# A decoder trunk on one core: input projection and low parts in another order, first two experts' rows by one-hot products, tables of slots later

## What is computed

```python
mod = silu(c) @ W_ada + b_ada                   # 6 x 1024: shift, scale, gate of both halves
h = rmsnorm(x) * (1 + scale1) + shift1
z = h @ W_in                                    # 4096 columns: q, k, v, pooled input, two gates
q, k = rmsnorm of each head of 64
A = block-sparse causal attention(q, k, v) @ W_attn_up
B = windowed means (2/4/8/16) minus the token, a linear map per group
x = x + gate1 * ((sigmoid(ga) * A + sigmoid(gp) * B) @ W_out)
h = rmsnorm(x) * (1 + scale2) + shift2
group = top-1 of 4;  expert pair = top-2 of the 8 in it      # routing of every token
x = x + gate2 * sum over 2 chosen experts of weight * (silu(h @ w1) * (h @ w3)) @ w2
```

## Time and profile before

| | us |
|---|---|
| median of 3 runs (lowest to highest) | 644.74 (643.94 to 645.98) |
| the profiled execution's own time | 648.95 |
| its span in the trace | 647.2 |
| PE busy | 579.7 (90% of the span) |
| DVE, ACT, POOL busy | 305.1, 161.3, 114.7 |
| bytes moved by DMA | 173.82 MB, mean 269 GB/s |

### The profile page before, as it was taken

The page is one execution under the profiler, slowest core; times in us unless marked ns, Lnnn a source line. Parts: engine busy times, 40 slices in busy tenths (PEclk is TensorE's granted clock), DMA queues, the critical chain, the costliest instruction groups (busy, mean ns, idle before and its releaser), DMA issues.

```text
span 647.2 us, 7332 instructions
## 1 busy us (share of the span) xinstructions
PE 579.7 (90%) x2786; PEld 343.2 (53%) x2786; DVE 305.1 (47%) x580; ACT 161.3 (25%) x348; POOL 114.7 (18%) x156
## 2 busy tenths in 40 slices
PE   3899699999999999999999999999986968889791
PEld 1554477777766677777788834333332323333241
DVE  0229876546646565249545385332221222253257
ACT  3034012234433434353303202121111111111110
POOL 3022242069300000064001011111111111101000
PEclk9899999999999999998999989999997988889897
DMA  8995944302581506030685695999999999999863
GB/s 308 396 353 212 338 159 163 131 19 111 201 319 52 210 1 260 1 131 0 265 337 244 235 386 177 369 423 418 419 420 422 419 422 419 420 419 421 337 276 130
DMA packets 42648, 173.82 MB, mean 269 GB/s; under 512 B 6396, under 2 KB 6460, under 8 KB 30836
## 3 DMA queue, kind: packets, MB, share of 16 engines
q1 hardware_dynamic: 35280, 159.40, 62.4%
q0 software_dynamic: 5744, 12.84, 5.4%
q10 hardware_dynamic: 1588, 1.10, 0.5%
HBM read 165.36 MB, written 15.74 MB: 280 GB/s over the span
## 4 chain that ended last, share of the span: by engine, by line
PE 72%; issue 10%; DMA 7%; DVE 6%; POOL 3%; SPq 1%; ACT 1%; ACTq 0%; DVEq 0%; POOLq 0%
PE bank L954 19%; PE bank L991 9%; PE bank L665 5%; PE bank L667 5%; PE bank L666 5%; DMA late<-in_w_ada_dram 3%; DMA late<-in_w_in_dram 3%; POOL ss L1954 3%; PE bank L932 3%; PE bank L849 2%; PE bank L787 2%; PE bank L851 2%; PE bank L850 2%; PE bank L689 2%; PE bank L716 1%
## 5 line engine op out<-in xcount | busy, mean ns | idle before, releaser
L954 PE MATMUL bank<-arena,hT 128*64 128x512 f32 x352 | 87.0, 637 | 16.8 <-issue 16.8
L665 PE MATMUL bank<-hT_high,w_in_parts 128*128 128x512 f32 x160 | 66.3, 414 | 0.0
L1694 DVE SCALAR_TENSOR_TENSOR g1b<-g1b,bank 128x256 f32<-128x256 f32 x16 | 6.7, 420 | 124.0 <-ACT g1b L1258 124.0
L667 PE MATMUL bank<-hT_high,w_in_parts 128*128 128x512 f32 x160 | 62.7, 392 | 0.0
L666 PE MATMUL bank<-hT_low,w_in_parts 128*128 128x512 f32 x160 | 62.4, 390 | 0.0
L954 PEld LDWEIGHTS bank<-arena,hT 128*64 128x64 f32 x352 | 26.3, 145 | 65.9 <-issue 64.5
L954 PE MATMUL bank<-late,hT 128*64 128x512 f32 x160 | 40.6, 653 | 9.2 <-issue 9.2
L991 PE MATMUL bank<-arena,g1b 128*64 128x512 f32 x176 | 40.2, 598 | 1.2 <-DVE acc L1718 1.2
L1995 POOL DMA_INDIRECT hT<-xn_scratch,gidx x16 | 16.5, 1029 | 136.9 <-PE bank L932 118.3
L1264 ACT COPY g1b<-bank 128x256 f32<-128x256 f32 x16 | 6.0, 372 | 131.3 <-PE bank L973 131.3
L1434 DVE TENSOR_REDUCE st<-bank 128x2 f32<-128x256 f32 (+3 forms) x16 | 13.2, 824 | 45.1 <-PE bank L691 45.1
(11 more groups left out here) (293 smaller groups left out, 1014.0 us busy)
## 6 DMA issues: line engine op xcount, KB each, us to landing
arena<-in_w_dram SPq DMA_DIRECT2D x58, 1024.0 KB, 26.2
late<-in_w_dram SPq DMA_DIRECT2D x30, 1024.0 KB, 25.6
late<-in_w_ada_dram SPq DMA_DIRECT2D x6, 2048.0 KB, 13.5
arena<-in_w_ada_dram SPq DMA_DIRECT2D x5, 2048.0 KB, 9.1
arena<-in_w_in_dram SPq DMA_DIRECT2D x4, 2048.0 KB, 11.0
late<-in_w_in_dram SPq DMA_DIRECT2D x4, 2048.0 KB, 18.1
arena<-in_w_dram SPq DMA_DIRECT2D x16, 512.0 KB, 8.4
y_scratch<-arena POOLq DMA_DIRECT2D x1, 4096.0 KB, 18.1
```

Of the source, the lines that this page charges most:

```text
L665: mm(bank[:, b, :], wH[:, b, k, :], hH[:, k, :], start=k == 0, stop=False)
L667: last = mm(bank[:, b, :], wL[:, b, k, :], hH[:, k, :], start=False, stop=k == 7)
L954: last = mm(bank[SLOTS * x:SLOTS * (x + 1), 2 + q % 2, :].rearrange("p (w f) -> p w f", w=2), xgT[q % 2][:, k, SLOTS * x:SLOTS * (x + 1)], ...
```

## The change

1. `CHUNKS`: chunk 2 of `W_in` is loaded before the pieces (3, 0) and (3, 1) of `W_ada`.
2. DVE: the low parts of the activations are written in two halves, k 0 to 3 in unit 2 (between `qk_norm` and `qk_scale`) and 4 to 7 at the start of unit 3; the low parts of chunk 2 likewise in the units 6 and 7. The pieces of `ada` stand later (units 1, 3, 4, 5, 7 to 11 in place of 1 to 10). `side("g1")` and `side("cols", 1)` stand two units later.
3. Projection: DVE writes the low parts of the first half of `W_out` behind the eight merged rows, no longer before and among them; ACT's high parts of it stand between the merged rows. The wait of `project` for `mL_ready` goes.
4. `xn2` is written chunk by chunk (element p * 8 + k of a row goes to place k * 128 + p), so what PE transposes later is contiguous.
5. The rows of the first pair (experts 0 and 1) are no longer gathered. DVE writes a float32 table `place0` (128 x 512) and PE multiplies `xn2` with it: `first_rows`, for each of 8 chunks k four 128x128 products, which at once give the transposed rows. Chunks 0 to 3 come before `gate_up(0)`, 4 to 7 in its middle. POOL's gathers begin with pair 1.
6. `slot_sums(0)` stands between the first products, `slot_sums(1)` inside `gate_up(0)`, `slot_sums(2)` behind the later k of `gate_up(1)`; the one-hot tables of the groups 1 and 2 move accordingly; four `keep_warm` calls become one.

```diff
         CHUNKS = [("ada", 1, 0), ("ada", 1, 1), ("ada", 0, 0), ("ada", 0, 1), ("in", 0), ("in", 1), ("ada", 2, 0),
-                  ("ada", 2, 1), ("ada", 3, 0), ("ada", 3, 1), ("in", 2), ("in", 3), ("ada", 4, 0), ("in", 6),
+                  ("ada", 2, 1), ("in", 2), ("ada", 3, 0), ("ada", 3, 1), ("in", 3), ("ada", 4, 0), ("in", 6),
...
+            def first_rows(ks):
+
+                for k in ks:
+                    for t in range(TT):
+                        last = mm(first_bank(k), xn2[:, t, P * k:P * (k + 1)],
+                                  place0[:, t].rearrange("p e s -> p (e s)"), start=t == 0, stop=t == TT - 1)
+                    if k % 2 == 1:
+                        last.then_inc(xt_ready if k == KT - 1 else x0_done, 1)
...
                 for k in range(KT):
+                    if q == 0 and k == KT // 2:
+                        first_rows(range(KT // 2, KT))
+                        pe.wait_ge(xgT_act, 1)
...
-                    if q == 0 and k == KT // 2 - 1:
+                    if q == 0 and k == KT - 3:
                         gather_transposes(1)
-                    if q == 1 and k < 3:
-
-                        slot_sums(2, IDX_GROUPS[2][4 * k:4 * k + 4])
-                    if q >= 1 and k == 3:
+                    if q == 0 and k == KT - 2:
+                        slot_sums(1)
+                    if q == 1 and k >= KT - 3:
+
+                        n = 4 * (k - KT + 3)
+                        slot_sums(2, IDX_GROUPS[2][n:n + 4])
+                    if q >= 1 and k == (KT - 1 if q == 1 else 3):
                         hidden_transposes(q - 1)
...
-            pe.wait_ge(idx_ready, 1)
-            gather_transposes(0)
-            keep_warm(2, 5)
+            keep_warm(1, 5)
+            pe.wait_ge(place0_ready, 1)
+            first_rows(range(2))
+            slot_sums(0)
+            first_rows(range(2, KT // 2))
...
-            out_weights_high(0, range(KT))
+            HIGHS = [range(0, 1), range(1, 3), range(3, 5), range(5, 7), range(7, 8)]
             for m in range(KT):
                 merged_high(m)
                 if m + 4 < KT:
                     up_high(m + 4)
+                if m < len(HIGHS):
+                    out_weights_high(0, HIGHS[m])
...
-            ADA_STEPS = {1: (0, early), 2: (1, early), 3: (2, early), 4: (2, later), 5: (3, early), 6: (3, later)}
-            ADA_AT = {1: [(0, later)], 2: [(1, later)], 9: [(4, early)], 10: [(4, later)], 16: [(5, early)],
+            ADA_STEPS = {1: (0, early), 3: (0, later), 4: (1, early), 5: (1, later), 7: (2, early)}
+            ADA_AT = {8: [(2, later), (3, early)], 9: [(3, later)], 10: [(4, early)], 11: [(4, later)], 16: [(5, early)],
...
+                    if u == U_K - 2:
+                        rows_low(range(0, 4))
+                    if u == U_V - 2:
+                        chunk_low(2, range(0, 4))
...
-            out_weights_low(0, range(0, 4))
             for m in range(KT):
                 side("A", m)
-                if m in (1, 2):
-                    out_weights_low(0, range(2 * m + 2, 2 * m + 4))
                 if m >= 1:
                     merged_low(m - 1)
             merged_low(KT - 1)
+            out_weights_low(0, range(KT))
...
-                    v.tensor_scalar(xn2[:, t, :], xs[:, t, :], st[:, 44 + t:45 + t], None,
+
+                    v.tensor_scalar(xn2[:, t, :].rearrange("q (k p) -> q p k", k=KT),
+                                    xs[:, t, :].rearrange("q (p k) -> q p k", k=KT), st[:, 44 + t:45 + t], None,
                                     ALU.mult).then_inc(xn2_ready, 1)
...
-            dve.wait_ge(xn2_stored, 16 * TT)
+            v.tensor_tensor(place0, rm[:, :, 0:2].unsqueeze(3).broadcast_to([P, TT, 2, SLOTS]),
+                            iota_s.unsqueeze(1).unsqueeze(1).broadcast_to([P, TT, 2, SLOTS]),
+                            ALU.is_equal).then_inc(place0_ready, 1)
...
             modulate_gathered(0)
+            one_hot(2, range(1))
...
+            dve.wait_ge(xt_ready, 1)
+            dve.wait_ge(xn2_stored, 16 * TT)
+            one_hot(1, range(TT))
             modulate_gathered(1)
-            one_hot(2, range(2, TT))
+            indices(1)
+            one_hot(2, range(1, 3))
+            dve.wait_ge(ab_done, 1)
+            one_hot(2, range(3, TT))
...
-            for q in range(STORED + 5):
+            for q in range(1, STORED + 5):
```

More of the change, by code:

```diff
@@ L194, in hybrid_trunk @@
         IDX_GROUPS = [range(0, 2), range(2, 4), range(4, PAIRS)]
-        idx_bank = lambda g: bank[:, (2, 2, 7)[g], :]
+        idx_bank = lambda g: bank[:, (4, 5, 7)[g], 192:]
+        LASTW = TT * PAIRS
+        first_bank = lambda k: bank[:, (0, 1, 3, 6)[k // 2], P * (k % 2):P * (k % 2 + 1)]
         HT = hT[:, :, :].rearrange("p a b -> p (a b)")
         PR = probs[:, :, :, :].rearrange("p a b c -> p (a b c)")
-        xg = carve(HT, 0, 2, D)
+        xg = [HT[:, 0:D], HT[:, D:2 * D]]
         xgT = [carve(HT, 3072, KT, P), carve(HT, 2048, KT, P)]
+        xg_of = lambda q: PR[:, D:2 * D] if q == 1 else xg[q % 2]
+        xgT_of = lambda q: carve(PR, 0, KT, P) if q == 0 else xgT[q % 2]
+        place0 = carve(g1b[:, :], 0, TT, 2, SLOTS)
         place = []
-        for qs, starts in zip(IDX_GROUPS, ([HT[:, 3072 + 128 * t:] for t in range(TT)],
-                                           [HT[:, 3584 + 128 * t:] for t in range(TT)],
-                                           [PR[:, 1024:], acc[:, 1, :], PR[:, 0:], g1b[:, :]])):
+        for qs, starts in zip(IDX_GROUPS, ([g1b[:, 512 + 128 * t:] for t in range(TT)],
+                                           [HT[:, 128 * t:] for t in range(TT)],
+                                           [acc[:, 1, :], HT[:, 3072:], g1b[:, :], PR[:, 0:]])):
             e_ = 2 * len(qs)
@@ L824, in _ @@
                     pv(a - 2)
-                if u in (4, 6):
-                    side("g1", u // 2 - 2)
-                if u == 9:
+                if u in (6, 8):
+                    side("g1", u // 2 - 3)
+                if u == 11:
                     side("cols", 1)
@@ L870, in router, with project_first @@
                 mm(o, ones[0:1, :], br[:, :], start=False, stop=True).then_inc(logits_ready, 1)
-            pe.wait_ge(side_drained, len(SIDE))
-            for t in range(TT):
+            def project_first():
+                for t in range(2):
+                    for k in range(KT - 1):
+                        if t == 0:
+                            pe.wait_ge(oH_ready, k + 1)
+                            pe.wait_ge(mH_ready, k + 1)
+                        mm(bank[:, t, :], mH[:, k, P * t:P * (t + 1)], w_out_high(0, k), start=k == 0, stop=False)
+                for t in range(2):
+                    ts = slice(P * t, P * (t + 1))
+                    if t == 0:
+                        pe.wait_ge(oH_ready, KT)
+                        pe.wait_ge(mH_ready, KT)
+                    mm(bank[:, t, :], mH[:, KT - 1, ts], w_out_high(0, KT - 1), start=False, stop=False)
+                    for k in range(KT):
+                        if t == 0:
+                            pe.wait_ge(mL_ready, k + 1)
+                        mm(bank[:, t, :], mL[:, k, ts], w_out_high(0, k), start=False, stop=False)
+                for t in range(2):
+                    for k in range(KT):
+                        if t == 0:
+                            pe.wait_ge(oL_ready, k + 1)
+                        last = mm(bank[:, t, :], mH[:, k, P * t:P * (t + 1)], oL[:, 0, k, :], start=False,
+                                  stop=k == KT - 1)
+                    last.then_inc(yo_done, 1)
+            pe.wait_ge(side_drained, len(SIDE) - 2)
+            project_first()
+            for t in range(2, TT):
                 project(t, 0)
@@ L1249, in modulate_gathered @@
                 for k in range(KT // 2, KT):
-                    last = sc.activation(xgT[q % 2][:, k, :], bank[:, 1, P * (k % 4):P * (k % 4 + 1)], ACT.Identity,
+                    if q == 0 and k == KT - 4:
+                        act.wait_ge(x0_done, 3)
+                    if q == 0 and k == KT - 2:
+                        act.wait_ge(xt_ready, 1)
+                    src = bank[:, 1, P * (k % 4):P * (k % 4 + 1)] if q else first_bank(k)
+                    last = sc.activation(xgT_of(q)[:, k, :], src, ACT.Identity,
                                          bias=ab2[:, 1, k:k + 1], scale=ab2[:, 0, k:k + 1])
@@ L1504, in _ @@
                     chunk_low(1, range(4 * u, 4 * u + 4))
-                if u in (5, 7):
-                    side("g1", u // 2 - 2)
-                if u == 10:
+                if u in (7, 9):
+                    side("g1", u // 2 - 3)
+                if u == 12:
                     side("cols", 1)
@@ L1684, in modulate_gathered @@
                 for k in range(KT // 2):
-                    last = v.tensor_scalar(xgT[q % 2][:, k, :], bank[:, k // 4, P * (k % 4):P * (k % 4 + 1)],
+                    if q == 0 and k % 2 == 0:
```

(3 more changed lines are left out.)

69 lines of the change are left out of this document (31 added, 38 removed).

## The result

The changed kernel took **630.21 us** (median of 4, 628.16 to 631.42) beside 645.36 us for the kernel before on the same chip (643.94 to 646.79): a ratio of 0.9751, interval 0.9713 to 0.9789. Two later sets gave ratios of 0.9730 and 0.9721, 17.4 and 18.0 us at 645.4.

The account below looks back on a forecast made before the run. It took a PE chain with DVE waits to bound the kernel up to the first pair, then the expert-weight DMA stream, whose start counts. Savings 8.8 + 0.3 + 1.2 = 10.3 us took 644.74 to 634.4 us; range 631 to 639.

Parts of the forecast that it names:

- part B: Around products A: `project` starts 2.0 us earlier, but a slow stretch inside it costs 1.7; 0.3 us saved.
- R1: Rival: no slow stretch of the clock in part B, behind PE's gap before `project`; 632.7 us, chance 0.20.
- Part A: Units 3 to 8: PE's idle gaps and slow clock go; 8.8 us saved, bounds 6.5 and 9.3.
- R2: Rival: DVE becomes the bound of units 4 to 8, 0.45 us a unit; 636.7 us, chance 0.14.
- Part C: Rows and first pair, up to the stream of expert weights: 1.2 us saved, bounds -4 and 2.5.
- (a): `xn2` write with a step of 512 bytes: 1.3 us against 0.754 contiguous, 0.5 us lost, bounds 0 and 1.5.
- R4: Rival: dearer strided `xn2` writes; the result turns at 3.5 us a write, 4.5 gives 648.9 us; chance 0.04.
- (b): DVE's write of the table `place0` for the first pair: about 0.65 us, ready at 380.5.
- (c): First-pair products at 0.29 us each: `gate_up(0)` starts at 385.6 (391.19 before), `ab_half` comes 5.6 us earlier.
- R3: Rival: the products of `first_rows` are dearer, 64 records costing 5.4 us more; 639.8 us, chance 0.12.
- (d): Rest of `gate_up(0)` with chunks 4 to 7: `ab_done` at 399.8, 0.35 us later than before.
- (e): Stream of expert weights: 1.9 us less transfer remains behind `ab_done`, minus 0.35 for its delay: 1.55 us saved.

Follow-up runs that it names:

- gap_filled: The change with `project` in its old order behind all drains, plus twelve products without use in PE's wait ahead of `project`; 633.37 us (ratio 0.9796).
- before_again: The kernel before, unchanged, run again for a second trace; 647.0 us median.
- a_only: The kernel before with part A alone (new load order, low parts in halves, `ada` pieces and two `side` calls later); 638.36 us (ratio 0.9874).
- c_only: The kernel before with part C alone (`xn2` written chunk by chunk, first pair's rows by products, tables later); 642.83 us (ratio 0.9953).
- b_only: The kernel before with part B alone (new order of DVE's and ACT's parts of `W_out`, and `project_first`); 640.74 us (ratio 0.9933).
- first_alone: The change with `project_first` kept, but DVE and ACT in their old order around the products A; 632.86 us (ratio 0.9781).
- pair1_behind: The change with pair 1's transposes and `slot_sums(1)` moved behind the last product of `gate_up(0)`; 627.85 us (ratio 0.9709).
- rows_in_order: The change with `xn2` written contiguously, as before, and read by PE with a step; 638.89 us (ratio 0.9893).

## Why the prediction was wrong, point by point

**The step that failed is the start of `project` in part B**: "DVE still has to drain it (1.4), write two merged low parts (1.4) and the first low part of `W_out` (0.6) before `project` can start". I walked the new order of DVE against the old order of PE and overlooked that the change reorders PE's products too. For the old order the walk was right: the start 3.58 us behind the last product A, the slow stretch, B's worth 0.1 (forecast 0.3), and the whole kernel 634.94 (forecast 634.4, so near in part by luck). With `project_first` PE waits for none of it and B is worth 5.5 to 5.8 us. This step alone takes the result out of the range: with 5.5 us in place of 0.3 the sum is 629.2, while C's error by itself would leave it at 632.6. The rival R1 had its price right (gap_filled: 1.6) and named the wrong kernel: here the gap itself is gone.

**Part A** held. 8.8 us were forecast. The first product A (L764; L754 before) starts at 275.73 instead of 285.32, 9.6 us earlier, in the two first traces, but against before_again (282.80) it is 7.1. The 1.7 us of slow clock at 79.3, which the sum counts, is thus lost in only some executions of the kernel before. Over all traces the transposes of unit 7 come at 106.7 on average without part A and at 97.2 with it, 9.5 earlier; a_only gains 8.1 (5.1 to 11.2) in the median. No idle time over 0.25 us stands in units 3 to 8; the 0.5 us kept for unit 7 was not lost. DVE was not the bound (R2).

**Part C**, 1.2 forecast, 3.0 measured (1.3 to 4.8, c_only).
(a) The strided write was taken at 1.3 us; it took 1.40. It is far from R4's 3.5. The prediction also works out 0.75 from the Trainium skill's rule on one-input operations (VectorE: DVE Perf Modes, "What auto-detection actually checks"). The measured time contradicts that figure for this access; whether the fast mode was off, or was on and the scattered writes cost the difference, no run here shows.
(b) `place0` took 0.69 (0.65).
(c) From the ranks to `gate_up(0)` 6.9 us were forecast and 5.48 measured: a record takes 0.12 us behind others, not 0.145. (The 0.94 us for six records in the earlier trace rows hold the last record's own 0.27; the five steps before it take 0.13 each.) R3 had the sign wrong. But what it replaces was also mis-seen. `project` ends at 360.84 in before and at 358.32 in before_again. POOL issues the first gather 21.8 us behind that in before and 20.0 in before_again, 1.8 earlier, yet PE has the rows 27.6 and 27.4 us behind it, at nearly the same distance. Timelines of POOL and PE, of before (first line; PE is in the earlier trace rows) and of before_again:

```profile
382.62 1.33 POOL L1995 DMA_INDIRECT hT<-xn_scratch,gidx  x1 [18.32 <-DVE gidx L1638]
```

```profile
378.31 1.33 POOL L1995 DMA_INDIRECT hT<-xn_scratch,gidx  x1 [16.55 <-DVE gidx L1638]
...
385.75 1.14 PE L932 MATMUL bank<-ident,hT 128*128 128x128 f32 x8 [2.44 <-DMA hT<-xn_scratch,gidx]
```

The same holds in all five traces that gather for pair 0: the gather is issued 20.0 to 21.8 us behind the end of `project`, the rows are there at 27.0 to 27.6. From the end of `project` to the first `gate_up` they take 29.8 to 30.3 us, or 31.7 and 31.8 with a slow stretch in the way (before_again, b_only); the kernels that multiply take 21.8 to 22.0, first_alone and pair1_behind 23.4 and 23.6 with a slow stretch, rows_in_order 27.4. That this wait is for the DMA engines, which are full until some 385 us with the last weights (share 1.02 from 380 to 385, 0.44 from 385 to 390 in before), fits these numbers; it was not tried by itself.
(d) From `gate_up(0)` to `ab_done` 14.2 us were forecast, 13.4 measured, for the same reason.
(e) The stream's 1.55 us were too many: from pair 1 to pair 15 the five traces without part C take 208.4 to 209.7 (mean 208.9), the seven with it whose rows and pair 1 stand as in the change 207.6 to 208.7 (208.1). That is 0.8. The larger part lies ahead of it: from the end of `project` to pair 1 the gathering kernels take 38.0 to 40.0 us (mean 38.9), the change and its like 35.2 to 35.4. So C's gain came by an earlier `ab_done` more than, as forecast, by less left to load behind a slightly later one. In the traces that is 3.7 + 0.8 = 4.5 us, of which the long slow stretch ahead of the ranks in three of the five gathering ones makes a part; in the median it is 3.0 (1.3 to 4.8). The DMA engines say the same, in busy tables of the 50 us from 10 us behind the end of `project`, of before, before_again, after and rows_in_order:

```profile
370.80:420.80 50.00, 48.68 (x261) 20.68 (x263) 28.10 (x94) 6.46 (x18) 6.33 (x6) 0.95 0.85 314
368.30:418.30 50.00, 45.73 (x249) 18.63 (x250) 28.09 (x94) 6.45 (x18) 6.32 (x6) 0.97 0.80 301
355.30:405.30 50.00, 47.73 (x310) 23.66 (x312) 30.21 (x100) 7.77 (x22) 7.04 (x6) 0.97 0.93 339
354.70:404.70 50.00, 47.86 (x252) 29.21 (x253) 27.20 (x93) 5.59 (x16) 5.06 (x4) 0.88 0.69 246
```

At 419 GB/s the change has 3.0 and 4.5 us more of the loads behind it at the end of this stretch than the two traces of before (an estimate from these rows).

**The signs named ahead.** Right: no gap and no slow clock in units 3 to 8; strided writes near 1.3; a break of some 3 us in the loads (share 0.14 from 379 to 382), then full. Off in size: 16 records in 2.05 (2.3 forecast), `ab_half` 7.0 us earlier against the ranks (5 to 6). Wrong: there is no gap before `project` and no slow stretch behind it, and `ab_done` is earlier against the ranks by 1.8 rather than the same.

## What to carry to other kernels

List what changed in the order of every engine that a chain crosses; a walk with one engine new and its partner old can get a wait right to 0.1 us (3.58 for 3.7) in a kernel that nobody runs. Where an engine waits at a joint, look for products that need only the finished operands, and bring them forward together with the producer's order: each alone brought 0.1 and at most 1.3 us here, both 5.5. Before two single traces are compared, list where their slow stretches fall. Choose the layout by the reader that repeats: 64 weight loads with a step lost 8 us to save four writes 0.65 us each.

## What the runs showed of the hardware

- Reading the 128x128 float32 weights of the products with a step of 32 bytes made the records of `first_rows` take 0.25 us instead of 0.12, but not those of the transposes of the same data (L868, 4.2 us for 32 either way), whose weight loads themselves were slower too (3.7 us in all contiguous, 4.2 with the step). Why the records differ stays open.
- A VectorE write of 1024 float32 with a step of 512 bytes took 1.40 us, against 0.754 contiguous.
- What a slow stretch costs depends on where it falls: ahead of the ranks one of 3.4 us cost 0.2 us (16.55 against 16.32), one of 6.8 us 1.5 to 1.8 (17.87 and 18.12); in `project` 3.4 us cost 1.6. An equal gap (1.90 and 1.92 us) had one behind it in a_only and none in first_alone, so the gap alone does not decide.
- The tail behind pair 15 has two lengths, 36.8 to 37.1 and 38.2 to 38.7 us, from one execution to the next of the same kernel: the longer where a slow stretch falls on the first 16 records of pair 15 (5.0 to 5.4 us for 3.65), in six traces of fourteen.
- A gather of 128 rows that was issued while bulk loads were under way had its rows used 27.0 to 27.6 us behind the end of `project` in five traces, whether it went out at 20.0 or at 21.8.
